# Three-block transformer on one core: a layer's queries and keys computed with tokens on the partitions, and two moves in the order of DVE

## What is computed

```python
u = rms_norm_2(h, norm_mix_g[i])
proj = u @ w_in[i]
a_in, c_x, c_b, c_c, q, k, v, gates = jnp.split(proj, split_at, axis=-1)
...
q = q.reshape(b_, s_, ATTN_HEADS, 2, ATTN_HEAD_DIM)      # 4 heads, 2 parts of 64
k = k.reshape(b_, s_, ATTN_HEADS, 2, ATTN_HEAD_DIM)
v = v.reshape(b_, s_, ATTN_HEADS, ATTN_V_DIM)
q1 = rms_norm_2(q[..., 0, :], q_norm_g[i])
q2 = rms_norm_2(q[..., 1, :], q_norm_g[i])
k1 = rms_norm_2(k[..., 0, :], k_norm_g[i])
k2 = rms_norm_2(k[..., 1, :], k_norm_g[i])
...
h = h + merged @ w_o[i]
m = rms_norm_2(h, norm_mlp_g[i])
h = h + jnp.square(jax.nn.relu(m @ w_up[i])) @ w_down[i]
e = rms_norm_2(h, norm_ple_g[i])
h = h + jax.nn.sigmoid(e @ w_ple_gate[i]) * (p[i] @ w_ple_proj[i])
```

## Time and profile before

| | us |
|---|---|
| median of 3 runs | 2596.42 (2596.28 to 2596.43) |
| profiled execution | 2596.76 |
| its span, first to last instruction | 2595.0 |
| PE busy | 2571.0 (99%) |
| DVE busy | 1568.3 (60%) |
| POOL busy | 1518.2 (59%) |
| ACT busy | 838.2 (32%) |

### The profile page before, as it was taken

The page is one execution under the profiler, slowest core; times in us unless marked ns, Lnnn a source line. Parts: engine busy times, 40 slices in busy tenths (PEclk is TensorE's granted clock), DMA queues, the critical chain, the costliest instruction groups (busy, mean ns, idle before and its releaser), DMA issues.

```text
span 2595.0 us, 32807 instructions
## 1 busy us (share of the span) xinstructions
PE 2571.0 (99%) x11675; PEld 2061.0 (79%) x11675; DVE 1568.3 (60%) x2096; ACT 838.2 (32%) x1157; POOL 1518.2 (59%) x1820
## 2 busy tenths in 40 slices
PE   8999999999999999999999999999999999999998
PEld 7767778888888877778888888887777888888887
DVE  7766774487474768856583442757874548344274
ACT  5444443233222333354321111134334432111112
POOL 7634446666666754555575665765454557565576
PEclk9999999999999999999999999999999999999999
DMA  5311113222222332222322222222222222222223
GB/s 206 114 66 49 52 64 130 92 87 97 99 95 97 114 104 77 71 97 81 106 97 99 97 97 97 94 101 104 67 80 98 82 106 94 102 97 97 97 91 120
DMA packets 36829, 247.44 MB, mean 95 GB/s; under 512 B 4464, under 2 KB 4848, under 8 KB 7792
## 3 DMA queue, kind: packets, MB, share of 16 engines
q1 hardware_dynamic: 34704, 238.57, 26.2%
q10 hardware_dynamic: 2016, 7.35, 0.8%
HBM read 243.81 MB, written 2.10 MB: 95 GB/s over the span
## 4 chain that ended last, share of the span: by engine, by line
PE 32%; POOL 30%; issue 22%; DVE 0%; POOLq 0%; ACT 0%; DVEq 0%
POOL w_lo L361 30%; PE bank L783 7%; PE bank L785 7%; PE bank L784 7%; PE both L783 3%; PE both L785 3%; PE both L784 3%; PE bank L818 0%; PE bank L1214 0%; PE both L1190 0%; POOLq L399 0%; POOLq L358 0%; PE bank L1202 0%; PE bank L1240 0%; POOL rg L387 0%
## 5 line engine op out<-in xcount | busy, mean ns | idle before, releaser
L361 POOL TENSOR_TENSOR w_lo<-raw,w_hi 128x256 fp32r<-128x256 f32 x1784 | 1495.9, 870 | 979.1 <-ACT w_hi L418 978.6
L418 ACT ACTIVATE w_hi<-raw 128x1024 fp32r<-128x1024 f32 x446 | 468.7, 1057 | 982.0 <-PE bank L785 481.7
L783 PE MATMUL bank<-a_hi,w_hi 128*128 128x512 f32 x1504 | 614.0, 408 | 0.0
L785 PE MATMUL bank<-a_hi,w_lo 128*128 128x512 f32 x1504 | 587.1, 390 | 0.0
L784 PE MATMUL bank<-a_lo,w_hi 128*128 128x512 f32 x1504 | 586.0, 390 | 0.0
L783 PEld LDWEIGHTS bank<-a_hi,w_hi 128*128 128x128 f32 x1504 | 282.5, 188 | 71.4 <-issue 16.1
L784 PEld LDWEIGHTS bank<-a_lo,w_hi 128*128 128x128 f32 x1504 | 282.9, 188 | 61.2 <-issue 7.4
L785 PEld LDWEIGHTS bank<-a_hi,w_lo 128*128 128x128 f32 x1504 | 282.3, 188 | 60.9
L783 PE MATMUL bank<-y_hi,w_hi 128*128 128x512 f32 x696 | 272.4, 391 | 0.0
L785 PE MATMUL bank<-y_hi,w_lo 128*128 128x512 f32 x696 | 270.9, 389 | 0.0
L784 PE MATMUL bank<-y_lo,w_hi 128*128 128x512 f32 x696 | 270.8, 389 | 0.0
(11 more groups left out here) (332 smaller groups left out, 3107.5 us busy)
## 6 DMA issues: line engine op xcount, KB each, us to landing
raw<-stream SPq DMA_DIRECT2D x223, 1024.0 KB, 4.8
h<-xT SPq DMA_DIRECT2D x8, 256.0 KB, 6.1
h<-xT ACTq DMA_DIRECT2D x1, 2048.0 KB, 8.3
outT<-h SPq DMA_DIRECT2D x8, 256.0 KB, 2.3
h<-decay ACTq DMA_DIRECT2D x1, 1024.0 KB, 4.9
h<-rope ACTq DMA_DIRECT2D x1, 1024.0 KB, 9.8
prob<-pT ACTq DMA_DIRECT2D x2, 512.0 KB, 4.5
par<-par ACTq DMA_DIRECT2D x2, 408.0 KB, 3.7
```

Of the source, the lines that this page charges most:

```text
L361: pool.tensor_tensor(w_lo[:, s, part], raw[:, s, part], w_hi[:, s, part], ALU.subtract).then_inc(lo_done, 1)
L418: act.activation(w_hi[:, s, cols], raw[:, s, cols], ACT.Copy).then_inc(hi_done, 1)
L783: pe.matmul(dst, w_hi[:, s, cols], rhs_hi(k), start=start and k == 0, stop=False)
L785: ins = pe.matmul(dst, w_lo[:, s, cols], rhs_hi(k), start=False, stop=stop and k == nk - 1)
```

## The change

It has three parts.

1. In a layer the query block and the key block are computed as the value block was: tokens on the partitions, in the order q, k, v, in `token_bank`. ACT squares each tile from PSUM, DVE adds up each group of 64 columns (L2001 in the new file), forms the factor of each token and group (L2003 to L2017, with a root on ACT), and scales the tiles into `m` (L2023). PE turns each head by four transposes into a bank that is free (`turn_heads`, in the second and third unit of the next block), and ACT copies it with the gain into `qn` or `kn` (`copy_head`). The sums with `ones2`, `qk_in` and `qk_out` are gone. `lam` is formed behind the value block.
2. In the first block's third step (j = 2) DVE forms the probabilities before it evicts the key unit, and PE's transposes of the third and the seventh step stand at k = 6 instead of k = 5.
3. After the last down-projection of a layer DVE only squares the last tile of `h`, evicts the first PLE unit, and then makes the last operand tile.

```diff
+        token_bank = [[bank[(i + 2) % 4][:, :] for i in range(QT)], [b[:, :] for b in (b_cmp, b_o, b_r0, b_r1)]]
...
+                def group_squares(block):
+                    for i in range(QT):
+                        if i < QT - 1:
+                            act.wait_ge(token_tile_done, layer * 9 + 3 * block + i + 1)
+                        else:
+                            act.wait_ge(unit_done, ul + 4 * block + 8)
+                        if i > 1:
+                            act.wait_ge(group_squares_read, layer * 8 + 4 * block + i - 1)
+                        act.activation((tile_b, tile_c)[i % 2], token_bank[block][i], ACT.Square)\
+                            .then_inc(group_squares_ready, 1)
+                def group_roots(block):
+                    act.wait_ge(group_sums_ready, layer * 2 + block + 1)
+                    act.activation(group_sum, group_sum, ACT.Sqrt, bias=eps).then_inc(group_roots_ready, 1)
+                def copy_head(block, hd):
+                    act.wait_ge(head_turned, layer * 8 + 4 * block + hd + 1)
+                    gain = (C2_QG, C2_KG)[block]
+                    act.activation((qn, kn)[block][:, hd, :], token_bank[block][hd], ACT.Copy,
+                                   scale=par[:, gain:gain + 1]).then_inc(head_copied, 1)
...
+                act.wait_ge(parameters_landed, layer * 16 + 32)
                 for j in range(8):
+                    if j in (0, 4):
+                        group_squares(j // 4)
                     ahead(ul + L_QK, j)
-                    if j > 0:
-                        tile_root((tile_b, tile_c)[(j - 1) % 2], (b_r0, b_r1)[(j - 1) % 2][:, :], 1.0 / 64)
+                    if j in (0, 4):
+                        group_roots(j // 4)
+                    if j in (1, 5):
+                        copy_head(j // 4, 0)
+                        copy_head(j // 4, 1)
+                    if j in (2, 6):
+                        copy_head(j // 4, 2)
+                        copy_head(j // 4, 3)
+                lam = small[:, 16:18]
+                act.wait_ge(to_activate, pre.due())
+                act.activation(lam, lam, ACT.Exp).then_inc(activated, res.up())
...
                     if k == 0:
-                        tile_root(tile_c, b_r1[:, :], 1.0 / 64)
                         load_table(ACT.Exp)
...
-                    if k == (5 if j % QT > 1 else 6):
+                    if k == (5 if j % QT == 3 else 6):
                         attention_transposes(j)
...
-                for u in range(4):
+                def turn_heads(block, heads):
+                    pe.wait_ge(evac, ul + 4 * block + 8)
+                    for hd in heads:
+                        for i in range(QT):
+                            ins = pe.transpose(token_bank[block][hd][:, i * P:(i + 1) * P],
+                                               m[:, 4 * block + i, hd * P:(hd + 1) * P], ident)
+                        ins.then_inc(head_turned, 1)
+                for block, u, i in itertools.product(range(3), range(4), range(QT)):
...
+                    if i == 0:
+                        pe.wait_ge(lo_done, (ul + 4 * block + u + 1) * LO_PARTS)
+                    if (block, u) == (0, 0):
+                        pe.wait_ge(evac, ul + i + 1)
+                    if (block, u, i) == (0, 2, 2):
+                        square_sum()
+                    if (block, u, i) == (1, 0, 3):
+                        pe.wait_ge(norm_sum_read, layer + 1)
+                    if (block, u) == (2, 0):
+                        pe.wait_ge(head_copied, layer * 8 + i + 1)
+                    if block > 0 and (u, i) == (1, 2):
+                        turn_heads(block - 1, (0, 1))
+                    if block > 0 and (u, i) == (2, 2):
+                        turn_heads(block - 1, (2, 3))
+                    dst = token_bank[block % 2][i]
+                    for o in range(2):
+                        k = 2 * u + o
+                        if block == 0 and i == 0:
+                            next_a(k)
+                        w = slice(cols.start + o * S, cols.start + (o + 1) * S)
+                        rows = slice(i * P, (i + 1) * P)
+                        pe.matmul(dst, a_hi[:, k, rows], w_hi[:, sl, w], start=k == 0, stop=False)
+                        pe.matmul(dst, a_hi[:, k, rows], w_lo[:, sl, w], start=False, stop=False)
+                        ins = pe.matmul(dst, a_lo[:, k, rows], w_hi[:, sl, w], start=False, stop=k == KD - 1)
+                    if i == QT - 1:
+                        ins.then_inc(unit_done, 1)
+                    elif u == 3:
+                        ins.then_inc(token_tile_done, 1)
...
-                    if i == 0:
-                        pe.wait_ge(retention_input_ready, rin.due())
+                    if s == 0:
+                        pe.wait_ge(head_copied, layer * 8 + 8)
...
-                for j in range(8):
-                    unit(ul + L_QK, j, 4, [bank4(j)], a_op(), 8,
-                         lambda k, j=j: square_sum((b_r0, b_r1)[(j - 1) % 2], ones2, (tile_b, tile_c)[(j - 1) % 2])
-                         if k == 3 and j > 0 else None)
...
-                    if k == 3 and slot == 0:
-                        square_sum(b_r1, ones2, tile_c)
...
-                if j > 0 and j != 6:
+                if j > 0 and j not in (2, 6):
                     unit_in(t, j - 1)
...
                 step_probs(t, j)
+                if j == 2:
+                    unit_in(t, 1)
...
                 leave(u0, j, V.tensor_tensor(h[:, n, :], bank4(j), h[:, n, :], ALU.add))
-                if g_col is not None:
+                if g_col is not None and (g_col, n) != (C2_PLE, KD - 1):
                     norm_tile(n, g_col, n == KD - 1)
...
-                rms()
+                V.wait_ge(root_ready, root.due())
+                V.reciprocal(rstd[:, :], rstd[:, :]).then_inc(norm_sum_read, 1)
+                V.wait_ge(norm_sum_read, layer + 1)
+                def tile_done(block, i):
+                    if i < QT - 1:
+                        V.wait_ge(token_tile_done, layer * 9 + 3 * block + i + 1)
+                    else:
+                        V.wait_ge(unit_done, ul + 4 * block + 8)
+                def grouped(x):
+                    return x.rearrange("p (g d) -> p g d", d=64)
+                def normed(block):
+                    for i in range(QT):
+                        V.wait_ge(group_squares_ready, layer * 8 + 4 * block + i + 1)
+                        V.tensor_reduce(group_sum[:, 8 * i:8 * i + 8], grouped((tile_b, tile_c)[i % 2]),
+                                        AX.X, ALU.add).then_inc(group_squares_read, 1)
+                    V.tensor_scalar(token_square, token_root, 1.0 / 64, None, ALU.mult)\
+                        .then_inc(vector_step, steps.up())
+                    V.wait_ge(vector_step, steps.now())
+                    V.tensor_tensor(token_square, token_square, token_root, ALU.mult)\
+                        .then_inc(vector_step, steps.up())
+                    V.wait_ge(vector_step, steps.now())
+                    V.wait_ge(group_squares_read, layer * 8 + 4 * block + 4)
+                    by_token = group_sum.rearrange("p (i g) -> p i g", g=8)
+                    V.tensor_tensor(by_token, by_token, token_square.unsqueeze(2).to_broadcast([P, QT, 8]),
+                                    ALU.mult).then_inc(group_sums_ready, 1)
+                    V.wait_ge(group_roots_ready, layer * 2 + block + 1)
+                    V.reciprocal(group_factor, group_sum).then_inc(vector_step, steps.up())
+                    V.wait_ge(vector_step, steps.now())
+                    factor = group_factor.rearrange("p (i g) -> p i g", g=8)
+                    V.tensor_tensor(factor, factor, token_root.unsqueeze(2).to_broadcast([P, QT, 8]), ALU.mult)\
+                        .then_inc(vector_step, steps.up())
+                    V.wait_ge(vector_step, steps.now())
+                    for i in range(QT):
+                        tile_done(block, i)
+                        leave(ul, 4 * block + i,
+                              V.tensor_tensor(grouped(m[:, 4 * block + i, :]), grouped(token_bank[block][i]),
+                                              group_factor[:, 8 * i:8 * i + 8].unsqueeze(2)
+                                              .to_broadcast([P, 8, 64]), ALU.mult))
+                normed(0)
+                normed(1)
...
+                    tile_done(2, i)
+                    leave(ul, 8 + i, V.tensor_scalar(vn[:, :, i, :], token_bank[0][i]
+                                                     .rearrange("p (h f) -> p h f", f=P),
+                                                     token_root[:, i:i + 1], None, ALU.mult))
...
+                square_tile(KD - 1, True)
                 for j in range(4):
+                    if j == 1:
+                        operand_tile(KD - 1, C2_PLE)
                     arrive(ul + L_PLE, j)
...
```

(26 more changed lines are left out.)

51 lines of the change are left out of this document (11 added, 40 removed).

## The result

The changed kernel takes **2581.33 us** (median of 4 runs, 2581.14 to 2581.87) against 2596.35 for the kernel before on the same chip. The ratio is 0.9942, with a 95% interval of 0.993 to 0.9954. The profiled execution took 2581.5 us, its span is 2579.7, 15.3 less than before.

The account below looks back on a forecast made before the run. PE, busy 2571.0 of 2595.0 us, was taken to set the time by what it issues and its waits. Terms -4.9 - 2.8 - 6.8 + 0.2 = -14.3 us gave 2582.1 from the median 2596.42; range 2579.5 to 2587.0.

Parts of the forecast that it names:

- Retention, -4.9: Attention heads: probabilities ahead of the key unit and later transposes remove the third step's stalls, leaving 0.6 us in head 0; -4.9 us.
- PLE, -2.8: Third PLE unit of both layers: moving the last operand tile behind the first eviction removes both stalls, -2.8 us.
- Sums against transposes, -6.8: Query and key blocks: 16 square sums go (-14.4 us), 64 transposes at a 0.114 pitch come (+7.6), net -6.8 us.
- The mixing units: Start of the mixing units: small waits of 1.2 us go because DVE is freer, counted only in the range's fast end.
- The turn, +0.2: First head transposes after layer 1's first token block: PE waits for DVE's scaled tiles, +0.2 us, bounds 0 and +2.
- POOL's w_lo, nothing: Weight work on POOL in the token blocks: keeps more than a unit of lead, so no cost.
- Busy time: Whole kernel: DVE's busy time lower by some 55 us, PE's lower by about the sum of the forecast gains.
- the first: Rival: the stall moves on to the fourth step or the turns, giving 2586.6 us; chance 0.15.
- The second: Rival: each new transpose costs its whole duration, 17.4 us in place of 7.6, giving 2591.9 us; chance 0.04.
- The third: Rival: slower grouped sums and scalings make the turn's wait the pace; 4.8 us slower, 2601.2, at 1.3 us extra each; chance 0.03.
- The fourth: Rival: the PLE stall stays in part because the second eviction is later, +0.5 to +1.8 us, up to 2583.9; no chance given.

## Why the prediction was right

The forecast was 2582.1, the result is 2581.33. The three parts gained by the mechanisms that were named, and the sizes were close, in part because small misses went both ways. Term by term, by the traces:

- *Retention, -4.9.* Measured -4.7. Heads 1 to 3 are as forecast (0.45, 1.74, 1.74 for 0.46, 1.69, 1.69). In head 0 the stall that stays was put at 0.6 and is 0.88 from start to start, so 0.8 was gained, not 1.1. The probabilities end at 120.79, where I had them at 120.63, and TensorE would have been there at 119.96, not 120.13. The mechanism (the compressed shift ahead of the maxima) is shown by the run that moved it. The shorter scalings, which I took from the rows and the Trainium skill's rule on the shared port pair (SBUF — State Buffer, Who interferes with whom), came: 0.48 and 0.48 where both start ahead of POOL, which begins at 259.00, and 0.80 and 0.76 beside POOL when only the place was changed.
- *PLE, -2.8.* Measured -3.0 in the trace, -2.8 alone. But 0.85 of layer 1's stall wasn't the tile's place alone. It went with either of the other parts as well, and where the others are changed the edit brings 2.3. I took a stall of 1.67 beside one of 0.82 for the same program place and never asked why they differ.
- *Sums against transposes, -6.8.* 16 sums at 0.90 were right (the eighth of each layer is gone too, in the mixing units). The transposes cost 7.1, not 7.6, by their doubling and by their own groups (0.89 each): their pitch is a little under the 0.114 that I read off four of them, and a group's ends cost 0.02 and not 0.04. The Trainium skill's figure (TensorE: Matmul & The Clock Gate, Part 4) of about 275 ns is the length of a record here too, 0.27, and no price: in a stream a transpose costs 0.11. The clock stayed at 1.0.
- *The mixing units* lost a wait of 0.22 in each layer that stood only in the range. That VectorE has no key or query tile to work on there any more would explain it, but no run isolates it.
- *The turn, +0.2.* My own terms, 1768.8 + 3.4 + 1.4 + 2.9, give 1776.5 and not 1776.6, just when TensorE was to come. It waits 0.36, in layer 1's first block alone, with the cause as forecast, ScalarE's squares behind a weight copy that waits for its transfer. The other three have 1.9 us of slack where I had 2.3.
- *POOL's w_lo, nothing.* I wrote that it keeps more than a unit of lead. In layer 1's fourth unit it has none: TensorE waited 0.31 for it before and waits 0.60 now. The run with the weights first took this wait away.
- *Busy time.* VectorE's fell by 62.3 us for the 55 that I named, with no effect on the time beyond these places. TensorE's was to fall by about the sum and fell by 8.4: a wait isn't busy time, so only what leaves its queue shows there, and what I wrote of it was wrong.

The rivals: the first stayed a trace of itself, 0.88 in head 0. The second is out by the doubling. The third, a turn's wait as the pace, needs more than 0.48 us for each of the four scalings before it shows in three of the blocks (1.9 / 4). In layer 1's first block it shows at once. At 0.72 it cost 7.3 us in all, where that rival's sum has 4 x 2.9 - 6.7 = 4.9: the slacks are smaller than it took, and in the trace the long stall also brought the clock down. The fourth didn't come: TensorE waits at neither the third nor the fourth PLE unit.

## What to carry to other kernels

Where one engine sets the end, price an edit by what it takes from that engine's queue and by the stalls that are left when the next wait is looked up, as 62 us of another engine's work were worth nothing by themselves. Parts of a change that were measured alone don't add up when two of them cure the same stall; take each one out of the whole as well. When a stall is twice as long at one of two places that run the same program, find out what the longer one has before it is booked as gain.

## What the runs showed of the hardware

- A stall of 3.58 us cost TensorE 1.5 us more behind it, at a granted clock of 0.62 in the mean of 4.5 us and of 0.50 in the windows from 1774 to 1776.5. It is one stall in one trace. Stalls of 1.67 and less left the clock at 1.0.
- A VectorE multiplication of 128x32 takes 0.19 to 0.20 us (36 times) or 0.77 to 0.78 (four times), and an upper half of 128x512 0.48 or 0.95, with a subtraction of POOL beside them; the half took 0.48 where it started 0.32 ahead of POOL's and 0.95 where it started 0.07 behind. Such tenths moved with edits far ahead. They made 0.6 us of difference at one wait, and 0.85 with a late start at another.
- A transpose of 128x128 in a row of eight costs TensorE's queue 0.11 us, while its record lasts 0.27.
- The port effects repeat with the kernel. The long PLE stall was 1.83 and 1.82 in two traces of the kernel before, and 0.98 in each of the three kernels that kept VectorE's order there and changed an earlier part.
